# A streaming encoder step: early loads of four feed-forward rows, and the doubling of the cached forgets moved behind the prompt's masks

## The reference

```python
def swiglu(h, w_in, w_out):
    gate, up = jnp.split(h @ w_in, 2, axis=-1)
    return (jax.nn.silu(gate) * up) @ w_out          # D_FF = 2816

def macaron_half(x, g_pre, g_post, w_in, w_out):
    return x + 0.5 * rms_norm(swiglu(rms_norm(x, g_pre), w_in, w_out), g_post)

def fox_block(q, k, v, cq, ck, qpos, kpos):           # forgetting attention, 8 heads of 64
    s = jnp.einsum('bqhd,bkhd->bhqk', q, k) * (HEAD_DIM ** -0.5)
    bias = cq[..., :, None] - ck[..., None, :]        # c: running sums of the log forgets
    p = jax.nn.softmax(jnp.where(kpos <= qpos, s + bias, -jnp.inf), axis=-1)
    return jnp.einsum('bhqk,bkhd->bqhd', p, v)
```

## Time and profile before

| | |
|---|---|
| median of 3 runs | 2697.7 us (2697.45 to 2700.3) |
| the profiled execution | 2698.24 us |
| its span | 2696.4 us, mean granted clock of PE 0.991 of full speed |
| PE matmul | 2599.3 us busy, 96% of the span |
| PE weight load | 2379.8 us, 88% |
| DVE | 1025.9 us, 38% |
| ACT | 841.4 us, 31% |
| POOL | 108.2 us, 4% |
| DMA | 210.8 MB, 78 GB/s over the span |

### The profile page before, as it was taken

One profiled execution on the slowest core, in us unless ns is written; L12 is line 12 of the kernel. 1 busy time (PEld: TensorE's weight loads), 2 busy tenths in 40 slices (PEclk: granted clock), 3 DMA queues, 4 the chain that ended last, 5 costly groups with the idle time before them and its releaser, 6 DMA issues. The chain is left out here.

```text
span 2696.4 us, 45912 instructions
## 1 busy us (share of the span) xinstructions
PE 2599.3 (96%) x19441; PEld 2379.8 (88%) x19441; DVE 1025.9 (38%) x1387; ACT 841.4 (31%) x1500; POOL 108.2 (4%) x104
## 2 busy tenths in 40 slices
PE   8999999999688999999999999999999999999998
PEld 8998997899457877998999799899979779989997
DVE  4232224433446756332232532322352473332324
ACT  4221223322545554322122432212243443221222
POOL 0000001000101221000000100000010010000001
PEclk9999999999899999999999999999999999999999
DMA  4231222223370002322222232222213212222222
GB/s 133 78 93 56 78 70 86 63 71 90 101 249 19 3 12 79 94 70 90 67 70 78 63 94 77 90 59 78 74 59 111 71 55 86 70 90 67 70 78 86
DMA packets 280404, 210.81 MB, mean 78 GB/s; under 512 B 24364, under 2 KB 236486, under 8 KB 280280
## 3 DMA queue, kind: packets, MB, share of 16 engines
q1 hardware_dynamic: 280280, 209.03, 25.8%
HBM read 201.94 MB, written 7.05 MB: 78 GB/s over the span
## 5 line engine op out<-in xcount | busy, mean ns | idle before, releaser
L459 PE MATMUL ps<-act_hi,pair_hi 128*128 128x320 f32 x2976 | 678.5, 309 | 0.0
L459 PE MATMUL ps<-act_lo,pair_hi 128*128 128x320 f32 x2976 | 678.0, 309 | 0.0
L459 PE MATMUL ps<-act_hi,pair_lo 128*128 128x320 f32 x2976 | 678.0, 309 | 0.0
L459 PEld LDWEIGHTS ps<-act_lo,pair_hi 128*128 128x128 f32 x2976 | 497.6, 188 | 0.0
L459 PEld LDWEIGHTS ps<-act_hi,pair_hi 128*128 128x128 f32 x2976 | 497.4, 188 | 0.3 <-issue 0.2
L459 PEld LDWEIGHTS ps<-act_hi,pair_lo 128*128 128x128 f32 x2976 | 497.6, 188 | 0.0
L421 DVE TENSOR_TENSOR pair_lo<-pair_raw,pair_hi 128x1024 fp32r<-128x1024 f32 x206 | 252.2, 1228 | 428.5 <-ACT pair_hi L417 428.0
L417 ACT ACTIVATE pair_hi<-pair_raw 128x1024 fp32r<-128x1024 f32 x206 | 216.0, 1052 | 516.1 <-PE ps L459 368.1
L507 PE MATMUL ps<-row_hi,hid_hi 128*128 128x512 f32 x880 | 346.3, 394 | 6.3 <-DVE row_lo L448 6.3
L507 PE MATMUL ps<-row_hi,hid_lo 128*128 128x512 f32 x880 | 345.1, 392 | 0.0
L507 PE MATMUL ps<-row_lo,hid_hi 128*128 128x512 f32 x880 | 345.0, 392 | 0.0
(11 more groups left out here) (387 smaller groups left out, 2459.7 us busy)
## 6 DMA issues: line engine op xcount, KB each, us to landing
pair_raw<-in_ffn_w_in_dram SPq DMA_DIRECT2D x176, 512.0 KB, 3.8
row_raw<-in_ffn_w_out_dram SPq DMA_DIRECT2D x176, 256.0 KB, 2.9
pair_raw<-in_even_w_in_dram SPq DMA_DIRECT2D x22, 512.0 KB, 3.9
norm_buf<-in_norm_g_dram SPq DMA_DIRECT2D x12, 512.0 KB, 4.4
y<-in_cache_fox_k_dram SPq DMA_DIRECT2D x4, 1024.0 KB, 6.9
y<-in_cache_fox_v_dram SPq DMA_DIRECT2D x4, 1024.0 KB, 5.6
norm_buf<-in_cache_fox_k_dram SPq DMA_DIRECT2D x4, 1024.0 KB, 7.8
norm_buf<-in_cache_fox_v_dram SPq DMA_DIRECT2D x4, 1024.0 KB, 5.4
```

The costliest lines, as they stand in the source:

```text
L459: mm = pe.matmul(ps[:, 2 * c + h, 0:HALF], w[c][:, k, :], a[:, k, h * HALF:(h + 1) * HALF], start=(k == 0 and w is pair_hi and a is act_hi ...
```

## The change

Two edits that don't touch each other.

**Four rows early.** In the second half of each feed-forward stage, rows 15 to 18 (of 0 to 21) are no longer loaded through `row_raw`, but into the four quarters of `xn_buf`, all four at once, in front of row 4, behind a wait for the stage's last turn. `sp_row` skips them; row 19 then follows row 13 in its buffer and row 20 row 14 (`last = i - 6`). ACT and DVE take rows 15 to 18 from `xn_buf`; ACT adds 32 to the counters of the two raw buffers for the rows that no longer come that way, and waits for all four early loads instead.

**The doubling behind the masks.** The copy of the cached forgets to the right half goes from `pool_streams` to the end of `pool_prompt`, and counts a semaphore of its own, which PE waits for in `forgets`. The loop of masks is written more simply; their order stays.

```diff
@@ -356,12 +356,13 @@
         s_mean, s_vsq, s_vroot, s_vinv, s_offset, s_v, s_v_gain, s_v_new, s_new_v = (sem(n) for n in (
             "v_mean", "v_squares", "v_root", "v_inverse", "v_offset", "v_normalised", "new_v_times_gain", "new_v_done",
             "new_v_stored"))
+        s_ffn_early = sem("ffn_early_rows_loaded")
         s_early, s_ub, s_ug, s_gu = (sem(n) for n in ("early_rows_loaded", "u_times_bias", "u_times_gain", "gain_part"))
         s_spatial, s_gated, s_ghi, s_glo = (sem(n) for n in ("spatial_products", "gated", "gated_hi", "gated_lo"))
         s_f_read, s_fall, s_call, s_callr = (sem(n) for n in (
             "f_rows_copied", "f_all_loaded", "c_all_summed", "c_all_read"))
         s_sel0, s_sel, s_qb0, s_qkn = (sem(n) for n in ("sel_all_cleared", "sel_all_set", "q_blocks_cleared", "qk_new_set"))
-        s_chi = sem("c_all_high")
+        s_chi, s_f_twice = sem("c_all_high"), sem("f_all_doubled")
         s_kc = [sem(f"k_cache{i}_loaded") for i in range(2)]
         s_vc = [sem(f"v_cache{i}_loaded") for i in range(2)]
         s_tk, s_kta, s_ktd = (sem(n) for n in ("cache_turned", "kt01_read", "kt23_read"))
@@ -400,10 +401,12 @@
             sp.dma_start(row_raw[i % 2][:, :], src).then_inc(s_row_raw[i % 2], 16)
 
         early_rows = {}
+        ffn_early = {before(f"ffn{f}", 1) + OUT_N * FF_K: {OUT_N * FF_K - TAIL + i: xn_buf[:, 512 * i:512 * i + 512]
+                                                           for i in range(4)} for f in range(4)}
 
         def early(i, base):
 
-            return early_rows[base].get(i) if base in early_rows else None
+            return early_rows.get(base, ffn_early.get(base, {})).get(i)
 
         def sp_early_rows(sp, base, rows, src_of):
             if rows[0] > 2:
@@ -433,6 +436,8 @@
                 act.wait_ge(s_row_raw[i % 2], (half_base + i // 2 + 1) * 16)
                 if early(i + 2, base) is not None:
                     act.sem_inc(s_row_raw[i % 2], 32)
+            elif base in ffn_early:
+                act.wait_ge(s_ffn_early, 16 * 4 * (list(ffn_early).index(base) + 1))
             elif i in (2, 9):
                 act.wait_ge(s_early, 16 * (8 * list(early_rows).index(base) + (4 if i == 2 else 8)))
             if base + i >= n:
@@ -590,6 +595,13 @@
                     sp_pair(sp, n0 + j, lambda half: w_in[:, :, bass.ds((c * FF_K + j) * P + half * D_FF, P)])
                 for i in range(OUT_N * FF_K):
                     n, k = i // FF_K, i % FF_K
+                    if c + 1 == FF_CHUNKS and i == 4:
+                        sp.wait_ge(s_tr, 5 * FFN_NORM[f] + TT)
+                        for e, raw in ffn_early[r0].items():
+                            k = e % FF_K
+                            sp.dma_start(raw, w_out[(c * FF_K + k) * P:(c * FF_K + k + 1) * P, 512:1024])\
+                              .then_inc(s_ffn_early, 16)
+                        k = i % FF_K
                     if i == OUT_N * FF_K - LOAD_AHEAD:
                         (first_pair_of(f"ffn{f}", c + 1) if c + 1 < FF_CHUNKS else load_next)(sp)
                     sp_row(sp, i, r0, h0, w_out[(c * FF_K + k) * P:(c * FF_K + k + 1) * P, n * 512:(n + 1) * 512])
@@ -1255,10 +1267,10 @@
 
             pool.wait_ge(s_att_const, 16)
             pool.wait_ge(s_cr, 16 * 4)
-            mask(0)
             for n in range(PSTEPS):
-                if n + 1 < PSTEPS:
-                    mask(n + 1)
+                mask(n)
+            pool.wait_ge(s_fall, 16 * NSEQ)
+            pool.tensor_copy(f_twice[:, :, 64:128], f_all).then_inc(s_f_twice, 1)
 
         def pe_prompt(pe):
             def scores(n):
@@ -1350,6 +1362,7 @@
                         mm.then_inc(s_tk, 1)
 
             def forgets():
+                pe.wait_ge(s_f_twice, 1)
                 for k in range(4):
                     pe.matmul(ps[:, 6, k * P:SEQ], f_twice[:, k, :], tri_ones[:, 0:SEQ - k * P],
                               start=(k == 0), stop=(k == 3))
@@ -1561,8 +1574,6 @@
             pool.wait_ge(s_logf, 1)
             pool.tensor_copy(logf_all[:, :].rearrange("p (b h) -> p b h", b=2 * NSEQ),
                              logf[:, 4:5, :].broadcast_to([P, 2 * NSEQ, FOXH]))
-            pool.wait_ge(s_fall, 16 * NSEQ)
-            pool.tensor_copy(f_twice[:, :, 64:128], f_all)
             pool.tensor_copy(k_new, qk[:, 4:8, SEQ:TOK]).then_inc(s_qkn, 1)
 
 
```

## The result

| | before | after |
|---|---|---|
| median, beside each other on one chip | 2697.57 us (4 runs, 2691.55 to 2700.3) | 2674.18 us (4 runs, 2668.57 to 2675.32) |
| ratio | | 0.9912, 95% interval 0.9897 to 0.9927 |
| the profiled execution | 2698.24 us | 2675.16 us |
| its span, mean granted clock | 2696.4 us, 0.991 | 2673.2 us, 0.994 |

The change is worth 23.4 us by the medians, 0.9%; the interval of the ratio spans 19.7 to 27.8 us. The forecast was 2669.1 us, a gain of 28.6: the direction and the range hold, the gain is 5.2 us short.

The account below looks back on a forecast made before the run. PE, busy 96% of the span, bounds the kernel, so only its idle or low-clock time can be gained. 16.5 + 3.2 + 7.3 + 1.6 = 28.6 us off 2697.7 gives 2669.1 us, range 2664.5 to 2675.

Parts of the forecast that it names:

- Prompt start: First bias step of the prompt starts at about 686.8 instead of 703.30, no longer behind POOL's late mask: 16.5 us.
- Clock in the first group: Prompt's first four steps take 9.81 us instead of 13.05, PE staying at 2.4 GHz without the stall: 3.2 us.
- Rival A: The clock falls at the prompt's thin start all the same: 2672.3 to 2673.9 us; chance 0.14.
- Forgets' wait: PE's forgets come some 20 us earlier, at 729, and the moved doubling, 0.40 us on POOL, costs nothing.
- Last rows: Stalls at the last seven rows of four feed-forward stages vanish: 6.3 us idle plus 0.26 restart each, 7.3 us.
- the spare of 2.6 us for row 21: In stage 0 row 21 is split by about 458.7, while PE wants it at 461.3.
- The ring: Ring of seven rows: row 21 may be split only when row 14's products are done, at 457.2 in stage 0.
- rival B: Stall at the feed-forward stages' end stays or moves as row 21 still comes late: 2678.0 us; chance 0.07.
- Clock in stage 2: The last-row stall in stage 2 lowered the clock, slowing the second tile's sum; without it 1.6 us come back.
- Early loads: Four extra DMAs, issued right behind rows 2 and 3, fall when no load is due and cost nothing.
- C: First mask waits for the c rows, as late as the forgets, so POOL's reorder fails: 2688.8 us; chance 0.03.
- D: Low clock returns and stays through prompt and streams, 41 us lost: 2715 us, slower than before; chance 0.02.

Follow-up runs that it names:

- the last experiment: Kernel before plus 154 small matmuls filling the 17 us wait, then 8 and 6 in the prompt's first gaps: 2695.84 us beside 2696.28, ratio 0.9997.
- Part 1 alone: Kernel before with only the doubling moved behind the masks, feed-forward rows as before: 2677.15 us beside 2696.23, ratio 0.9926.
- the two with the filled start: Changed kernel plus 28, 4 and 12 small matmuls before and between the program's first turns, run twice: 2667.79 us (0.9896) and 2671.54 us (0.9906).
- the two kernels with the prompt filled in: Small matmuls in the prompt's first gaps: added to the changed kernel, 2674.07 us (0.9913); to before, with 154 in the 17 us wait, 2695.84 us (0.9997).
- Part 2 alone: Kernel before with only the four rows loaded early, POOL's order as before: 2691.43 us beside 2696.23, ratio 0.9977.
- the run with 140 matmuls: Kernel before plus 140 small matmuls in PE's 17 us wait ahead of the third scores: 2699.90 us beside 2699.51, ratio 1.0011.

## Why the prediction was right, and 5 us too far

- **Prompt start, 16.5 us:** 16.1. The chain is the predicted one: mask long done (669.90; I had said about 672), DVE waits 0.49 us for the scores, PE 0.88 us for DVE (I had said about 0.4: its next scores need the bias of both heads, and the second ends at 686.74 + 0.69).
- **Clock in the first group, 3.2 us:** this step failed. The size is right, as the last experiment shows. The step said that PE comes out of the row products at 2.4 GHz and keeps it, so that all of it comes back. In three profiled executions of the changed kernel 0.8, 1.7 and 1.7 us came back; in Part 1 alone and in the two with the filled start all 3.2. Rival A, with a chance of 0.14, is what happened in the three of the changed kernel, in a weaker form: the fall is later and shorter than behind the stall, not absent. Its counter-argument (716 to 720 at 1.00 with PE busy 3.45) was read from a thicker stretch: the prompt's first steps have 2.2 to 2.5 us of 4. The estimate by the Trainium skill ("TensorE: Matmul & The Clock Gate", section "Terms"), 5.1 us for this stretch, was too high also for the whole effect: 3.2 measured, as part of each step isn't PE's.
- **Forgets' wait, 0:** right; 5.7 us of cover.
- **Last rows, 7.3 us:** 7.3, stage by stage, but with less room than I said. Against PE the spare of 2.6 us for row 21 holds: its split was done at 459.96, and PE, 1.2 us late since the program's start, wanted it at about 462.5. The ring opened at some 458.6, less that 1.2 at 457.4; I had 457.2. The load was misjudged: it landed at 458.50, with 1.2 off at 457.3, where I had 455.5. Row 19 was split not at 452.6 but at 456.0 (454.8 with 1.2 off), since DVE has the four low parts of rows 15 to 18 (4.69 us) and the pair's (2.35 us) ahead of it, and the prediction counted only ACT's work there. So the DMA isn't out of the path, as rival B's answer had it: it ties with the ring, here and in stages 1 and 2, within 0.1 us. It cost nothing.
- **Clock in stage 2, 1.6 us:** this step failed too, though the number is there in this pair. The step said that the stall brought the clock down. Part 1 alone and the two kernels with small matmuls in the 17 us kept that stall and had the 1.6 us all the same. So the term is a fall that the kernel before happened to have in its profiled execution, and getting it in this pair was luck.
- **Early loads, 0:** right. They were issued as said, behind rows 2 and 3:

```profile
397.53 0.93 SPq L401 DMA_DIRECT2D row_raw<-in_ffn_w_out_dram  x2
398.50 1.85 SPq L602 DMA_DIRECT2D xn_buf<-in_ffn_w_out_dram  x4
410.08 0.93 SPq L401 DMA_DIRECT2D row_raw<-in_ffn_w_out_dram  x2
```

  and no step of DVE is later for it.
- **Rival B** (tail stall stays) and **C** (masks wait for the c rows) are refuted by the rows above, **D** (low clock persists) by 708.21 - 698.40 = 9.81 us.
- **The sum.** The designed terms, 16.1 + 7.3 = 23.4, equal the gain of the medians, and that they do so to the tenth is chance: the three ratios of the changed kernel make it 23.7, 25.9 and 22.4 us. The 4.8 us of clock were counted at their full size. In the profiled pair 2.4 of them came back (0.8 and 1.6) and 2.5 more between the prompt and feed-forward 1, while 4.7 were lost elsewhere: 1.2 at the start, 1.6 at 1054 to 1067, 1.9 in the gated MLP. That the falls elsewhere come with other gaps had been written down, and given a chance of 0.04; they should have been a term with a mean. The execution at 2668.78 shows that 2669.1 is within what this kernel does, and not where its median lies.

What stays open: why the medians of the two kernels with the prompt filled in (0.9913; 0.9997) show nothing of the 1.6 to 3.2 us that each profile has at the place. In the first, the profile shows the streams' waits for cached keys taking it back; why those waits are longer there (2.89 and 3.09 us with the prompt filled in, 2.6 in Part 2 alone, at most 1.7 in the other profiles) no run tells. Beyond that, a spread of some 4 us either way can hide it; the intervals (±1.3 per mille, 3.5 us, in the first) can't tell. One fall for one saved was not shown.

## What to carry to other kernels

Read an in-order queue from the wait backwards and ask of each instruction ahead of the awaited one whether the awaited one needs it: here one copy of 0.40 us, behind a DMA that it alone needed, held three engines for 17 us. A stall at the end of a ring of loads can be moved by loading some rows into a buffer that lies idle, and its worth is the idle time plus the restart, term by term. A low clock behind a stall is no certain gain of removing the stall: look at how busy PE is in the steps that follow; if they are thin, count half of it, and look for the same dip in more than one execution before it becomes a term. Small matmuls into an unread bank kept the clock up at the place each time they covered the gaps, and brought the program's start forward by 0.7 to 2.3 us, but only the second showed at all in the medians. And when an engine gets more to do ahead of a load's release, here DVE's four splits ahead of row 19's, put that work into the load's chain.

## What the runs showed of the hardware

- The granted clock falls to 0.50 also without a long stall: after gaps of 1.64 and 0.96 us (at 706.5 in the run with 140 matmuls), and in after at 2069.0 and 2075.8, in stretches where PE is recorded as busy 4.00 of 4 us. Busy is not the same as full there: from 2065.66 PE ran 16 matmuls of a single column in 1.94 us. The first of the two falls has its like in the second and third execution of the same kernel (at 2062.5 and 2066.1 of theirs), the second hasn't: which falls come is a matter of the execution, and the times of one kernel spread over 9 us (2668.6 to 2678.0), the longer ones at the lower mean clock.
- At the program's start the column of the granted clock says 1.00 while products of one form are 0.21 us apart, and 0.12 later; the durations tell what the column doesn't. The Trainium skill (same page, section "Part 1: The HAM clock gate") says that the number of slow matmuls at a kernel's start differs from run to run; the trace agrees: 17 products in after, and 12 each in the second and third profile of the same kernel.
- A mean granted clock is no measure between kernels: the run with 154 small matmuls has 0.997 against 0.991 of before and is faster by 1.9 us in the profiled pair and 0.4 in the median. Part of that is the idle stretch, where a low clock costs nothing; not all of it, as the sum of the table, which counts only PE's busy time, falls by more as well (13.9 to 6.5 us).
